# Rebuilding the chain from the router's product to the list of experts in a one-core transformer kernel

## What is computed

```python
def moe_ffn(h, w_router, router_bias, w_gu, w_down, w_sh_gu, w_sh_down):
    scores = jax.nn.sigmoid((t @ w_router).astype(f32))
    choice = scores + router_bias.astype(f32)
    group_score = lax.top_k(choice.reshape(-1, N_GROUPS, per_group), 2)[0].sum(-1)
    _, gidx = lax.top_k(group_score, TOPK_GROUPS)
    ...
    _, eidx = lax.top_k(jnp.where(emask, choice, -jnp.inf), TOP_K)
    w = jnp.take_along_axis(scores, eidx, axis=-1)
    w = w / jnp.sum(w, axis=-1, keepdims=True) * ROUTED_SCALE
    ...
    sg, su = jnp.split(t @ w_sh_gu, 2, axis=-1)
    shared = (jax.nn.silu(sg) * su) @ w_sh_down
    return (routed + shared).reshape(B, S, D)
```

## Time and profile before

| | us |
|---|---|
| median of 3 runs | 1614.06 |
| lowest and highest | 1613.41, 1623.69 |
| the profiled execution, whole | 1611.18 |
| the profiled execution, span from the first to the last instruction | 1609.5 |

### The profile page before, as it was taken

How to read it: one execution, slowest core, us unless ns; L and a number is a source line. 1 busy time by engine, 2 the same in 40 slices (tenths; PEclk the granted TensorE clock), 3 DMA queues, 4 the chain that set the end, 5 groups by cost and what they waited for, 6 DMA issues and landing times.

```text
span 1609.5 us, 27392 instructions
## 1 busy us (share of the span) xinstructions
PE 1522.5 (95%) x10546; PEld 1020.3 (63%) x10546; DVE 738.6 (46%) x1256; ACT 489.8 (30%) x758; POOL 45.7 (3%) x97
## 2 busy tenths in 40 slices
PE   6999999999989899999999999988989999989987
PEld 6999978666777799997844455463434444434442
DVE  5555447255655565554599756361211222222212
ACT  5333343143333543334001271112222222222221
POOL 6000010100000000001000000000000000000000
PEclk9999999999999899999999999979999999999999
DMA  9846393321436645627544333329898997888984
GB/s 321 291 157 205 108 324 113 115 70 53 170 106 237 233 157 181 212 104 277 199 157 144 132 117 131 138 82 366 336 404 295 344 353 248 347 338 302 354 327 171
DMA packets 156218, 350.92 MB, mean 218 GB/s; under 512 B 12656, under 2 KB 57920, under 8 KB 155713
## 3 DMA queue, kind: packets, MB, share of 16 engines
q1 hardware_dynamic: 152464, 343.05, 59.4%
q0 software_dynamic: 1792, 3.09, 0.6%
q10 hardware_dynamic: 1840, 3.17, 0.6%
HBM read 579.89 MB, written 2.16 MB: 362 GB/s over the span
## 4 chain that ended last, share of the span: by engine, by line
PE 69%; DVE 12%; DMA 9%; SPq 4%; ACT 3%; issue 2%; DVEq 0%; ACTq 0%
PE bank L669 16%; PE bank L2857 8%; PE bank L648 7%; DVE arena L2342 6%; PE bank L2885 6%; PE bank L2143 5%; PE bank L1073 4%; DMA ring<-in_w_exp_down 4%; DMA ring<-in_w_exp_gu 3%; PE bank L1803 3%; PE bank L2791 3%; SPq L3108 2%; PE bank L2771 2%; PE bank L1082 2%; PE bank L1820 2%
## 5 line engine op out<-in xcount | busy, mean ns | idle before, releaser
L669 PE MATMUL bank<-x_high,w_high 128*128 128x256 f32 x704 | 200.5, 285 | 5.8 <-DVEq L252 5.8
L669 PE MATMUL bank<-x_low,w_high 128*128 128x256 f32 x704 | 200.4, 285 | 0.0
L669 PE MATMUL bank<-x_high,w_low 128*128 128x256 f32 x704 | 199.3, 283 | 0.0
L741 DVE TENSOR_TENSOR w_low<-ring,w_high 128x2048 fp32r<-128x2048 f32 x60 | 137.3, 2292 | 77.0 <-ACT w_high L706 76.8
L2143 PE MATMUL bank<-ring,xT 128*128 128x512 f32 x384 | 166.0, 593 | 1.8 <-ACT arena L2500 1.8
L669 PEld LDWEIGHTS bank<-x_high,w_high 128*128 128x128 f32 x704 | 133.8, 190 | 7.3 <-issue 6.6
L669 PEld LDWEIGHTS bank<-x_high,w_low 128*128 128x128 f32 x704 | 135.0, 192 | 0.0
L669 PEld LDWEIGHTS bank<-x_low,w_high 128*128 128x128 f32 x704 | 133.7, 190 | 0.7
L706 ACT ACTIVATE w_high<-ring 128x2048 fp32r<-128x2048 f32 x60 | 114.5, 1912 | 60.8 <-PE bank L648 59.2
L2143 PEld LDWEIGHTS bank<-ring,xT 128*128 128x128 f32 x384 | 72.6, 190 | 91.9 <-issue 91.8
L2885 PE MATMUL bank<-ring,arena 128*32 128x512 f32 x1024 | 118.8, 605 | 8.5 <-DMA ring<-in_w_exp_down 8.5
(11 more groups left out here) (563 smaller groups left out, 2432.3 us busy)
## 6 DMA issues: line engine op xcount, KB each, us to landing
ring<-in_w_exp_gu SPq DMA_DIRECT2D x512, 512.0 KB
ring<-in_w_exp_down SPq DMA_DIRECT2D x128, 1024.0 KB
ring<-in_w_in SPq DMA_DIRECT2D x42, 768.0 KB, 6.1
ring<-in_ffn_w_gate SPq DMA_DIRECT2D x22, 1024.0 KB, 5.8
ring<-in_ffn_w_up SPq DMA_DIRECT2D x22, 1024.0 KB, 8.5
ring<-in_ffn_w_down SPq DMA_DIRECT2D x21, 1024.0 KB, 10.0
ring<-in_w_ada SPq DMA_DIRECT2D x24, 768.0 KB, 5.8
ring<-in_w_in SPq DMA_DIRECT2D x21, 512.0 KB, 7.8
```

What stands on the lines that cost most here:

```text
L669: ins = pe.eng.matmul(bank[:, k * S:(k + 1) * S], ff_w[f][w][:, c, k, :], (x_high, x_low)[x][:, c, :], start=c == 0 and i == 0, stop=c == ...
L741: v.eng.tensor_tensor(low[:], raw_piece((base + a) % NS, p), high[:].bitcast(F32), ALU.subtract).then_inc(low_set[p], 1)
```

## The change

Nothing of the result is changed; the same experts with the same gates come out.

- PE: the first `gate2` rows are made before `xT` is waited for, then the two `tri`/`ones` products, then the router's product, then the second `gate2` rows. `shared_gu(0, 0)` and `shared_gu(1, 0)` follow, and the wait for empty banks stands behind them. `shared_gu(0, 1)` moves ahead of the wait for `blocks_set`, `shared_gu(1, 1)` behind the transposes of the gates, and the four pairs of down products, which stood together, are spread: one ahead of the tables of seats, three behind them.
- ACT loads the sigmoid's table with an instruction on one column, and takes the router's product from its bank, without DVE's copy. Nothing of DVE is waited for.
- DVE sets four columns, `starts`; finds the two best of each group by pairwise `max` and `min` over all 16 groups at once (ten instructions) in place of 16 `max`; ranks the groups of both tiles at once; copies `count1` and `seat` out of the bank behind `mask_set`, and only then gives the bank back; makes the starts of the lanes with one instruction in place of four. `token1`, the second `seat` and the shared expert's hidden product stand behind the tables.

```diff
-            pe.get()
-            wait(router_loaded, 32)
-            b = pe.q.fill()
-            for t in range(T):
-                for c in range(DC):
-                    ins = mm(ps[b][:, t * N_EXP:(t + 1) * N_EXP], xT[:, c, t * P:(t + 1) * P],
-                             router[:, c, :], start=c == 0, stop=c == DC - 1)
-            mm(ps[b][:, 128:256], ones, tri, start=True, stop=True)
-            ins = mm(ps[b][:, 256:258], tri, ones[:, 0:2], start=True, stop=True)
-            ins.then_inc(psum_full, 1)
-            for n in range(2):
+
+            def gate2_rows(n):
                 wait(gate2_parts_set, n + 1)
                 b = pe.q.fill()
...
-            pe.q.emptied()
+
+            gate2_rows(0)
+            pe.get()
+            wait(router_loaded, 32)
+            b = pe.q.fill()
+            mm(ps[b][:, 128:256], ones, tri, start=True, stop=True)
+            mm(ps[b][:, 256:258], tri, ones[:, 0:2], start=True, stop=True)
+            for t in range(T):
+                for c in range(DC):
+                    ins = mm(ps[b][:, t * N_EXP:(t + 1) * N_EXP], xT[:, c, t * P:(t + 1) * P],
+                             router[:, c, :], start=c == 0, stop=c == DC - 1)
+            ins.then_inc(psum_full, 1)
+            gate2_rows(1)
...
             shared_gu(0, 0)
+            shared_gu(1, 0)
+            pe.q.emptied()
             wait(mask_set, 1)
...
+            shared_gu(0, 1)
             wait(blocks_set, 1)
             mm(ps[7][0:32, 256:512], seat[few, 0, 0, 0:1].to_broadcast([N_EXP, 32]),
                blocks[few].rearrange("p a b c -> p (a b c)"), start=True, stop=True)\
                 .then_inc(experts_full, 1)
-            shared_gu(0, 1)
             wait(gates_set, 1)
             for t in range(T):
                 ins = tr(ps[6][few, S + t * P:S + (t + 1) * P], gates[:, t, :], ident[:])
             ins.then_inc(tables_full, 1)
-            shared_gu(1, 0)
+            shared_gu(1, 1)
+            wait(shared_hid, 1)
+            shared_down(0, 0)
             wait(tables_set, 1)
...
             ins.then_inc(seats_full, 1)
-            shared_gu(1, 1)
+            shared_down(1, 0)
             wait(shared_hid, 2)
-            shared_down(0)
-            shared_down(1).then_inc(shared_done, 1)
+            shared_down(0, 1)
+            shared_down(1, 1).then_inc(shared_done, 1)
```

```diff
-            b = v.q.take()
-            do(cp(left, view(ps[b], 0, (T, N_EXP))))
-            do(cp(count1, ps[b][:, 128:256]))
-            do(cp(seat[:, 0, :, 0], ps[b][:, 256:257].to_broadcast([P, COLS])), psum_free)
-            v.pass_on(2)
-            v.ask()
-            do(cp(token1[:, 0:P], count1))
-            do(ts(token1[:, P:S], count1, float(P), None, ALU.add))
-            do(ts(seat[:, 1, :, 0], seat[:, 0, :, 0], float(P), None, ALU.add))
-            v.answer()
+            v.pass_on(1)
+            logits = v.hand()
+            v.pass_on(1)
+            for i, at in enumerate((-1.0, -2.0, float(COLS), COLS + 1.0)):
+                do(e.memset(starts[:, i:i + 1], at))
             wait(router_loaded, 32)
+            wait(scores_set, 1)
             do(tt(choice, scores, every(bias64, T), ALU.add))
-            for t in range(T):
-                for g_ in range(GROUPS):
-                    do(e.max(best[:, t, g_, :], choice[:, t, g_ * PER:(g_ + 1) * PER]))
-            do(tt(gsum, best[:, :, :, 0], best[:, :, :, 1], ALU.add))
...
+            do(tt(high4, pairs[:, :, 0:4], pairs[:, :, 4:8], ALU.max))
+            do(tt(low4, pairs[:, :, 0:4], pairs[:, :, 4:8], ALU.min))
+            do(tt(high2, high4[:, :, 0:2], high4[:, :, 2:4], ALU.max))
+            do(tt(mid2, high4[:, :, 0:2], high4[:, :, 2:4], ALU.min))
+            do(tt(low2, low4[:, :, 0:2], low4[:, :, 2:4], ALU.max))
+            do(tt(low2, low2, mid2, ALU.max))
+            do(tt(high1, high2[:, :, 0], high2[:, :, 1], ALU.max))
+            do(tt(mid1, high2[:, :, 0], high2[:, :, 1], ALU.min))
+            do(tt(low1, low2[:, :, 0], low2[:, :, 1], ALU.max))
+            do(tt(low1, low1, mid1, ALU.max))
+            do(tt(gsum.rearrange("p t g -> p (t g)"), high1, low1, ALU.add))
...
+            do(tt(more, other, mine, ALU.is_equal))
+            do(tt(more, more, before, ALU.mult))
+            do(tt(larger, other, mine, ALU.is_gt))
+            do(tt(more, more, larger, ALU.add))
...
             do(tt(left, left, choice, ALU.not_equal), mask_set)
+            do(cp(count1, ps[logits][:, 128:256]))
+            do(cp(seat[:, 0, :, 0], ps[logits][:, 256:257].to_broadcast([P, COLS])), logits_read)
+            v.give_back(1)
...
+            do(ts(start[few].rearrange("p b x -> p (b x)"), starts[few], share[few, 0:1],
+                  0.5 / COLS - 0.5, ALU.mult, ALU.add))
...
             do(cp(gatesT[few], ps[6][few, S:2 * S]), tables_set)
+            do(cp(token1[:, 0:P], count1))
+            do(ts(token1[:, P:S], count1, float(P), None, ALU.add))
+            do(ts(seat[:, 1, :, 0], seat[:, 0, :, 0], float(P), None, ALU.add))
+            for f in range(2):
+                wait(shared_silu, f + 1)
+                do(tt(sh_hid[:, f], sh_sg[:, f], ps[4 + f][:, S:2 * S], ALU.mult), shared_hid)
```

```diff
-            a.get()
-            do(f(scores, left, ACT.Sigmoid))
-            a.put()
+            do(f(stat[:, 30:31], eps[:], ACT.Sigmoid))
+            do(f(scores, view(a.full(a.hand()), 0, (T, N_EXP)), ACT.Sigmoid), scores_set)
             for n in range(2):
-                f(gate2[:, n * 512:(n + 1) * 512], ps[a.take()][:], ACT.Copy).then_inc(psum_free, 1)
+                gate2_rows(n)
```

More of the change, by code:

```diff
@@ L2928, in vec_part @@
[L2928 to L2936 removed]
+            pairs = choice.rearrange("p t (g e) -> p (t g) e", g=GROUPS)
@@ L3027, in vec_part @@
             choose(0)
-            for f in range(2):
-                wait(shared_silu, f + 1)
-                do(tt(sh_hid[:, f], sh_sg[:, f], ps[4 + f][:, S:2 * S], ALU.mult), shared_hid)
             choose(1)
```

48 lines of the change are left out of this document (25 added, 23 removed).

## The result

| | before | after |
|---|---|---|
| median, kernels timed side by side (15 runs each) | 1616.61 | 1608.74 |
| lowest and highest | 1612.37, 1623.69 | 1604.72, 1614.93 |
| the profiled execution, whole | 1611.18 | 1609.89 |
| its span | 1609.5 | 1608.2 |

The ratio after / before is 0.9948, with a 95% interval of 0.9937 to 0.9960: 8.4 us less, between 6.5 and 10.2. By the prediction's bound of 1% that is within 1%, as forecast; the forecast itself was 6.4 us less, 1607.7 us, and the measured 1608.74 lies in its range. By the medians alone the fall is 7.9 us.

What follows compares the result with a forecast made beforehand. Until 1152 the wire (DMA transfers), not PE, sets the pace, fed by a relay that makes the expert list. List 2.8 plus closed hole 3.6 gives 6.4 us off the median 1614.06: 1607.7 us, range 1603 to 1612.5.

Steps and rivals of the forecast that it cites:

- The list: Rebuilt chain that picks experts and makes the list: it reaches SP 2.8 us earlier, bounds 1.15 to 4.2.
- pairwise operations: Two best of each group on DVE: 2.5 us in place of 3.49 with MAX8, so -1.0 us.
- the two copies: The router's bank is given back only behind two copies after the mask: +0.6 us on the path.
- the moved product: `shared_gu(0, 1)` ahead of the last sum, partly at low clock: 5.7 us, within 5.4 to 6.4.
- The warm engine: Rival: `shared_gu(0, 1)` runs at full clock, list 4.2 us earlier, time 1606.3 us; chance 0.14.
- The hole: DMA falls to 117 GB/s from 1093 to 1098, lane 3 waiting for the shared expert; closing it gives 3.6 us.
- the spare: `shared_done` at 1085.4, with 3.6 us to spare before lane 3 must be released, by 1089.
- The wait before step 0's down product: PE idles about 6.6 us there in place of 3.00; the product costs the same 6.5 us.
- carried along: All that follows 1152 comes earlier by what the state at 1152 comes earlier, and no more.
- Slower: Rival: PE becomes the one waited for, its clock at half from 1043; list 10.4 us later, 1624.5 us; chance 0.04.
- given back: Rival: the hole stays or its gain is lost before 1152; only the list counts, 1611.3 us; chance 0.16.

Runs made afterwards that it cites:

- the weaker wait: The change with the counting products in bank 1, so PE counts without waiting for the two copies behind the mask; executed once, 1609.34 us.
- spread: The kernel before with only PE's shared-expert products spread and the hidden products behind the tables, as in the change; ratio to before 0.9976.
- fill_count: The change plus five unused products behind the second `shared_gu`, filling PE's idle stretch ahead of the count; ratio to before 0.9954.
- tok_behind: The change with `tok_low` moved from the head of DVE's chain to behind the shared expert's hidden products; ratio to before 0.9928.
- grouped: The change without the spread products: the shared expert's products stand where before had them; ratio to before 0.9982.
- warm: The change plus eight unused products ahead of the loop over the steps, before step 0's gate-up; ratio to before 0.9965.
- gu_behind: The change with `shared_gu(0, 1)` put back behind the last sum (L2821); ratio to before 0.9936.
- max8: The change with 16 MAX8 and one addition again in place of the eleven pairwise operations; ratio to before 0.9960.
- best: The change with `shared_gu(0, 1)` behind the last sum, `tok_low` behind the tables, counts in another bank, first hidden product earlier; ratio to before 0.9933.
- late_table: The change without ACT's early sigmoid on one column that loads the table; executed once, 1609.40 us.

## Why the prediction held, and where its steps were off

**The list, -2.8.** Every term of its sum stands within 0.3 us: `choice` -2.6 for -2.4; memsets 0.44 for 0.4; pairwise operations 2.47 for 2.5; the two copies +0.61, isolated by the weaker wait; the moved product 5.98 for 5.7, within the 5.4 to 6.4; L2821 0.61 for 0.6. The step that could have gone the other way was the clock at the moved product, and there the rows won over the rule as the prediction read it. Read so, the Trainium skill's "TensorE: Matmul & The Clock Gate", section "Loop structure matters more than you think", would have had the product run at full clock, and the list 4.2 us earlier. But of its two reasons the prediction leaned on the wrong one. It named the idle stretch ahead of the count, and it argued from the small products: the clock is low since PE has only these there. In spread, fill_count and tok_behind PE has the same small products and the moved one takes 3.62 us; what they lack is the idle stretch ahead of the count. So these runs agree with what the Trainium skill says there of waits between products, though its example is a long wait for a DMA ahead of every product and here it was one wait of 1.8 to 3.4 us for DVE; the change is a kernel that has such a wait. The warm engine was a rival for the wrong kernel: fill_count has it, at -1.8 us.

**The hole, -3.6.** Right in mechanism and size. Landing less list is 37.5 us (37.3 to 37.6) in the ten traces in which the shared expert ended early enough, 41.1 and 41.3 in those of before and 41.5 in grouped: the closed hole is worth 3.6 to 4.0 us. (The fourteenth is warm, with 39.2 and a part of the hole.) `shared_done` was 46.0 from the norm; the prediction's 1085.4 in the trace of before is 45.8. The two halves, tried apart, showed 3.4 and 4.0 at the landing. Only the spare was smaller than the 3.6 us that the prediction gave it. The shared expert ended 15.0 us behind the start of the list's copy in the change; in gu_behind it was 17.4, and nothing was lost, but in warm 18.2, 3.3 us more than in the change, and 1.7 us were.

**The wait before step 0's down product.** Predicted 6.6 us, measured 1.89 and 3.32: a miss. The step that failed had gate-up of step 0 done two microseconds behind lane 3's last piece, near 1099 (59.4 from the norm); it ran 10.03 and 8.51 us, after its own wait for weights (2.77 and 2.55 us) and in stretches at 0.74 and 0.82 granted clock, and was done at 63.9 in the change's first trace. Two things were left out: gate-up could start only at 53.9, and 7.07 us of full clock from there end at 61.0, 1.6 us later than predicted; the low clock added the other 3.0. The error was harmless, since the wire sets the landing, as the prediction had said: a slower product took the place of a longer wait. "The same 6.5 us" for the down product held in the second trace (6.30), not in the first (3.64).

**That it is carried along.** Up to the landing, yes. At step 3 the change is 6.6 to 7.8 us ahead (104.4 and 104.8 against 111.4 and 112.2). At the end of the span the traces scatter more: 569.9 and 571.0 for before, 565.8 and 564.7 for the change, 5.2 us ahead in the mean. The traces show where the scatter comes from. From the start of one step's gate-up to the next is 14.7 us for 17 to 20 of the 32 steps in each of the 14 traces, and the same in both kernels; it is longer in steps that wait for weights, and by how much varies from trace to trace, in part with the clock that the product behind the wait gets. The down product of step 6 in the trace of before and, second row, of after:

```profile
1215.88 3.64 PE L2885 MATMUL bank<-ring,arena 128*32 128x512 f32 x32 [1.36 <-DMA ring<-in_w_exp_down]
1210.76 5.34 PE L2893 MATMUL bank<-ring,arena 128*32 128x512 f32 x32 [1.99 <-DMA ring<-in_w_exp_down]
```

The second has the stretch at 0.50 from 1211.6 to 1214.8, the last of PE's stretches above. Step 6 took 24.3 us there and 22.0 before, and step 21, where the down product took 5.34 us for 3.64 as well, 22.5 and 21.3. Together that is 3.6 us, next to the 3.7 us that the change loses in this pair of traces between step 3 (-7.8) and the end (-4.1). In its second trace both down products ran in 3.64 us.

**Whether the landing's gain becomes time.** No pair of kernels can tell, but the nine that were timed can together. Gained at the landing against the mean of the two traces of before, and gained in time by the ratio (of 1616.6 us):

| kernel | landing, us | time, us |
|---|---|---|
| grouped | 3.5 | 2.9 |
| spread | 4.1 | 3.9 |
| max8 | 5.4 | 6.5 |
| warm | 5.9 | 5.7 |
| after | 6.6 | 8.4 |
| gu_behind | 8.1 | 10.3 |
| fill_count | 8.3 | 7.4 |
| tok_behind | 10.8 | 11.6 |
| best | 10.9 | 10.8 |

No kernel is further than 2.2 us from giving in time what it gained at the landing, and the sum over all is 67.5 us for 63.6. That bears out "carried along", as closely as these timings can.

**What stays open.** The time fell by 8.4 us, 6.5 to 10.2; the prediction's 6.4 is just outside. No trace of the two kernels shows the 2 us beyond it: from the landing to the end of the span it was 495.0 and 495.8 us in the traces of before and 497.2 and 496.2 in those of the change. Whether the change has a small gain more or its 15 runs were lucky isn't shown.

**Luck in the absolute time.** The forecast 1607.7 us and the measured 1608.74 are closer than the forecast deserves. It started from 1614.06, a median of 3 runs, where before has 1616.61 in 15, and took off 6.4 us where it was 8.4: the two errors cancel in part. That a change of less than 16 us can't be measured here was wrong too: the interval is 3.7 us wide.

**Slower, or given back.** Neither came. The low clock after waits is there in every trace of the change. Taken away ahead of step 0 (warm) it gave no time that could be measured, and PE then waits for the wire in any case; ahead of the list (fill_count) it gave 1.8 us at the landing, and less than the timing can tell.

## What to carry to other kernels

Split a relay from the wire behind it: find the last event that releases transfers and the hole in GB/s that waiting for it leaves, and price the two apart; they added up here (3.4 and 4.0 us tried alone, 6.4 together). A product behind an idle stretch of PE cost up to 1.7 times its length here (6.2 us for 3.62), so look first at that stretch and not at the small products around it. The chain that ended last names what released a transfer, and not whether the wire stood empty meanwhile: take that from GB/s. And once a wait is closed, ask who decides next: three edits worth 0.5, 1.6 and 4.3 us at the landing were worth 4.4 together, since DVE's own work was all that was left.

## What the hardware did that was not expected

- The same 16 instructions of 128x256 in float32 took 3.62 us with at most 0.24 us of idle time ahead of the count and 5.1 to 6.2 us with 1.8 to 3.4 us of it. The granted clock doesn't fall in the idle stretch itself: in after it is 1.00 from 1061.0 to 1064.6, which holds the idle time and the count, and 0.50 from 1064.8, under the moved product.
- ACT's load of the sigmoid's table took 1.28 us, and its instruction began 0.01 us behind it (late_table). Where the instruction that needs it waited for PE, the load waited too (late_table, 1053.18, released by L2745).
- From the list's copy to the landing of the first 12 MB it was 37.5 us, within 0.3, in ten traces with different clocks and orders on PE: once the wire was fed without a gap, its time didn't depend on them.
